# First block: the depthwise convolution wholly on TensorE in two halves, softmax in place in four buffers, layer norm sums inside the last two pairs of heads

## What is computed

```python
h = rms_norm(x, norm1_g);  a, gate, q, k, v = split(h @ w_in)
u = a * sigmoid(gate)                                # (256, 512)
y = depthwise_conv(u, dw_kernel, width=31) + dw_bias # centred, over tokens
y = silu(layer_norm(y, conv_ln_g, conv_ln_b))        # over the 512 channels
q, k = rms_norm per head;  8 heads of 64
p = softmax(q k^T / 8 + learned bias inside a 16-column window)
x = x + concat([y, p v]) @ w_out
x = x + (silu(h2 @ w_gate) * (h2 @ w_up)) @ w_down   # h2 = rms_norm(x, norm2_g)
```

## Time and profile before

| What | Value |
|---|---|
| Median of 3 runs | 1096.16 us (1095.68 to 1097.02) |
| Profiled execution | 1097.69 us, its span 1095.9 us |
| PE busy in the span | 1056.6 us (96%) |
| DVE, ACT, POOL busy | 680.8, 526.3, 69.6 us |
| Mean granted TensorE clock | 0.983 of full |
| DMA | 183.94 MB, mean 168 GB/s |
| Chain that ended last | PE 90%, DVE 4%, ACT 3%, DMA 1%, issue 1% |

### The profile page before, as it was taken

How to read it: one execution, slowest core, us unless ns; L and a number is a source line. 1 busy time by engine, 2 the same in 40 slices (tenths; PEclk the granted TensorE clock), 3 DMA queues, 4 the chain that set the end, 5 groups by cost and what they waited for, 6 DMA issues and landing times.

```text
span 1095.9 us, 19080 instructions
## 1 busy us (share of the span) xinstructions
PE 1056.6 (96%) x7498; PEld 972.8 (89%) x7501; DVE 680.8 (62%) x1035; ACT 526.3 (48%) x681; POOL 69.6 (6%) x80
## 2 busy tenths in 40 slices
PE   6997799999999999999999999989999999999997
PEld 5984589999998999999899899889999989999996
DVE  5995556555555677758655554565767676555554
ACT  6464554434445643546544444365344556444433
POOL 0000000000000115300000000003080000000000
PEclk7999899999999999999999999999999999999999
DMA  9971145455554655238465554645542584656520
GB/s 294 275 223 40 38 146 200 157 190 193 189 164 135 204 162 155 78 115 300 128 226 194 189 185 132 204 150 185 168 141 67 176 296 137 210 170 202 166 93 39
DMA packets 140146, 183.94 MB, mean 168 GB/s; under 512 B 5861, under 2 KB 125367, under 8 KB 140087
## 3 DMA queue, kind: packets, MB, share of 16 engines
q1 hardware_dynamic: 139576, 182.99, 52.8%
q10 hardware_dynamic: 511, 0.14, 0.1%
HBM read 180.90 MB, written 1.56 MB: 167 GB/s over the span
## 4 chain that ended last, share of the span: by engine, by line
PE 90%; DVE 4%; ACT 3%; DMA 1%; issue 1%; SPq 0%; ACTq 0%; DVEq 0%
PE col L490 19%; PE col L491 19%; PE col L492 19%; PE acc L490 9%; PE acc L491 9%; PE acc L492 9%; DVE wlo L1204 2%; ACT whi L900 1%; PE acc L661 1%; DVE y L1310 1%; DMA raw<-in_w_in 1%; PE acc L648 1%; PE acc L627 1%; PE col L679 1%; PE acc L557 1%
## 5 line engine op out<-in xcount | busy, mean ns | idle before, releaser
L1204 DVE TENSOR_TENSOR wlo<-raw,whi 128x2048 fp32r<-128x2048 f32 (+1 forms) x179 | 390.0, 2181 | 198.0 <-ACT whi L900 196.9
L490 PE MATMUL col<-uhi,whi 128*128 128x256 f32 (+1 forms) x1392 | 398.6, 286 | 4.7 <-DVE ulo L1231 3.9
L492 PE MATMUL col<-uhi,wlo 128*128 128x256 f32 (+1 forms) x1392 | 395.7, 284 | 0.0
L491 PE MATMUL col<-ulo,whi 128*128 128x256 f32 (+1 forms) x1392 | 395.7, 284 | 0.0
L900 ACT ACTIVATE whi<-raw 128x2048 fp32r<-128x2048 f32 (+1 forms) x179 | 325.0, 1820 | 121.6 <-PE acc L492 71.9
L490 PEld LDWEIGHTS col<-uhi,whi 128*128 128x128 f32 (+1 forms) x1392 | 267.6, 192 | 9.5 <-issue 6.0
L491 PEld LDWEIGHTS col<-ulo,whi 128*128 128x128 f32 (+1 forms) x1392 | 267.8, 192 | 1.5
L492 PEld LDWEIGHTS col<-uhi,wlo 128*128 128x128 f32 (+1 forms) x1392 | 267.8, 192 | 0.0
L490 PE MATMUL acc<-whi,mhi 128*128 128x512 f32 x376 | 148.5, 395 | 6.4 <-DVE wlo L1204 6.3
L491 PE MATMUL acc<-wlo,mhi 128*128 128x512 f32 x376 | 147.2, 392 | 0.0
L492 PE MATMUL acc<-whi,mlo 128*128 128x512 f32 x376 | 146.9, 391 | 0.0
(11 more groups left out here) (246 smaller groups left out, 1033.0 us busy)
## 6 DMA issues: line engine op xcount, KB each, us to landing
raw<-in_w_in SPq DMA_DIRECT2D x52, 1024.0 KB, 5.4
raw<-in_w_mlp_up SPq DMA_DIRECT2D x32, 1024.0 KB, 5.7
raw<-in_w_mlp_down SPq DMA_DIRECT2D x32, 1024.0 KB, 4.9
raw<-in_w_gate SPq DMA_DIRECT2D x11, 1024.0 KB, 5.4
raw<-in_w_up SPq DMA_DIRECT2D x11, 1024.0 KB, 5.4
raw<-in_w_down SPq DMA_DIRECT2D x11, 1024.0 KB, 4.8
raw<-in_w_mix_out SPq DMA_DIRECT2D x8, 1024.0 KB, 5.7
raw<-in_w_out SPq DMA_DIRECT2D x4, 1024.0 KB, 9.6
```

The lines of the kernel that those rows point to most:

```text
L490: pe.matmul(out, l_hi, r_hi, start=start, stop=False)
L491: pe.matmul(out, l_hi, r_lo, start=False, stop=False)
L492: return pe.matmul(out, l_lo, r_hi, start=False, stop=stop)
L1204: dve.tensor_tensor(wlo[:, u.buf, 0:size], raw[:, u.slot, 0:size], whi[:, u.buf, 0:size].bitcast(F32), ALU.subtract).then_inc(w_lo, 1)
```

## The change

All four chunks of the convolution go to PE, in two halves of two chunks with the same `shifted` and `kst` buffers. The first half's shift copies are issued by SP between the loads of units 8 and 9, and its 64 matmuls follow unit 6 on PE. The second half's copies wait for the first half's matmuls and follow the load of unit 11; its stationaries are built by DVE after unit 8's turn in its list; its matmuls lie in pairs 0 and 1. The taps of DVE are gone. The tap gathers move from ACT's queue to SP's, behind unit 1, and carry twice the rows; their transpose stands after unit 0. Softmax runs in place: maximum, exponential and scaling use the same one of four buffers, and ACT no longer waits for a turn before an exponential. The mean's matmuls move into pair 2, the variance's into pair 3, the subtraction and the squares beside them. ACT splits unit 12 before the pairs and unit 13 right after the sigmoids; DVE's low halves stay after the pairs and after the convolution's low halves. ACT's own load of the square root's table before the wait for the variance is dropped. `last_rows` asks for units 12 and 13 and their inputs one after the other.

The core of the diff:

```diff
             load(a_unit(0), w_in[:, :, A_COLS[0]:A_COLS[0] + COLS])
             for j in range(1, A_OUT):
                 load(a_unit(j), w_in[:, :, A_COLS[j]:A_COLS[j] + COLS])
+                if j == 1:
+                    for s in range(SHIFTS):
+                        n = (TAPS - s + SHIFTS - 1) // SHIFTS
+                        sp.dma_start(krow[0:GROUPS * n, SHIFT_CH * s:SHIFT_CH * s + SHIFT_CH], taps_of(s, n)).then_inc(taps_in, 16)
+                    sp.dma_start(krow[GROUPS * (TAP_SETS - 1):GROUPS * TAP_SETS, SHIFT_CH * (SHIFTS - 1):P], taps_of(TAPS - 1, 1))\
+                        .then_inc(taps_in, 16)
+                if j == 8:
+                    shift(0)
...
+            def shift(half):
+                sp.wait_ge(glu, half + 1)
+                if half:
+                    sp.wait_ge(conv_ps, 2)
+                for s in range(SHIFTS):
+                    for q in range(SHIFTS):
...
                 load(a_unit(A_OUT + i), w_out[:, 2 * r:2 * r + 2, :])
                 if i == 1:
...
+                    shift(1)
...
+            def convolve(c):
+                for g in range(TAP_SETS):
                     for q in range(SHIFTS):
+                        mm = pe.matmul(CONV_BANK[c][SHIFT_CH * q:SHIFT_CH * q + SHIFT_CH, 0:T], kst[2 * (c % 2) + q // 2][:, g, q % 2, :],
+                                       shifted[:, SHIFTS * (c % 2) + q, SHIFTS * g:SHIFTS * g + T], start=g == 0, stop=g == TAP_SETS - 1)
+                mm.then_inc(conv_ps, 1)
...
+                if j == 0:
+                    tap_transposes()
+                if j == 6:
+                    pe.wait_ge(kst_ok, 1)
+                    pe.wait_ge(shift_in, 16 * SHIFTS * SHIFTS)
+                    convolve(0)
+                    convolve(1)
                 if j == 7 or j == 8:
                     n = j - 7
                     pe.wait_ge(qk_tok, n + 1)
+                    if n:
+                        pe.wait_ge(conv_sb, 2)
                     turn((qtok, ktok)[n], n)
             for p in range(HEADS // 2):
                 if p + 1 < HEADS // 2:
                     score_pair(0, p + 1)
                 if p == 0:
                     pe.wait_ge(evac, A_OUT)
-                    pe.wait_ge(kst_ok, 1)
-                    pe.wait_ge(shift_in, 16 * SHIFTS * SHIFTS)
+                    pe.wait_ge(kst_ok, 2)
+                    pe.wait_ge(shift_in, 2 * 16 * SHIFTS * SHIFTS)
                 else:
                     value_pair(0, p - 1)
-                if p < len(CONV_AT):
-                    convolve(CONV_AT[p - 1] if p else 0, CONV_AT[p])
+                if p < 2:
+                    convolve(2 + p)
+                elif p == 2:
+                    pe.wait_ge(conv_sb, KA)
+                    for c in range(KA):
+                        mm = pe.matmul(MU[:, 0:T], ones[:], y[:, c, :], start=c == 0, stop=c == KA - 1)
+                    mm.then_inc(ln_mu, 1)
+                else:
+                    pe.wait_ge(ln_sq, 2)
+                    for c in range(KA):
+                        mm = pe.matmul(VAR[:, 0:T], ones[:], lnsq[:, c, :], start=c == 0, stop=c == KA - 1)
+                    mm.then_inc(ln_var, 1)
                 turn_probs(0, 2 * p)
                 turn_probs(0, 2 * p + 1)
...
             def exps(a, h):
                 act.wait_ge(s_max, HEADS * a + h + 1)
-                if h >= 2:
-                    act.wait_ge(p_ps, HEADS * a + h - 1)
                 for t in range(NT):
+                    p = expo[h % 4][:, t, 0:keys(a, t)]
+                    act.activation(p, p, ACT.Exp, bias=nmx[:, h % 4, t:t + 1], accum_out=den[:, h % 4, t:t + 1]).then_inc(s_exp, 1)
...
+                    if j == 0:
+                        act.wait_ge(kx_ps, 1)
+                        act.activation(kx[:], col[2][:, 0:TAP_SETS * GROUPS], ACT.Copy).then_inc(kx_sb, 1)
...
             exps(0, 1)
+            split(a_unit(A_OUT + 2))
             for p in range(HEADS // 2):
...
                     if e == 0 and p >= 1:
                         o_split(0, p - 1)
-            o_split(0, 3)
-            for p in range(2):
-                f = slice(2 * p, 2 * p + 2)
-                act.wait_ge(ln_xc, p + 1)
-                act.activation(lnsq[:, f, :], y[:, f, :], ACT.Square).then_inc(ln_sq, 1)
-            split(a_unit(A_OUT + 2))
-            act.activation(sd[:, 2:3], eps[:, 0:1], ACT.Sqrt)
+                for c in range(2 if p == 2 else 0):
+                    f = slice(2 * c, 2 * c + 2)
+                    act.wait_ge(ln_xc, c + 1)
+                    act.activation(lnsq[:, f, :], y[:, f, :], ACT.Square).then_inc(ln_sq, 1)
             act.wait_ge(ln_var, 1)
             act.activation(lnsd, VAR[:, 0:T], ACT.Sqrt, bias=eps[:, 0:1]).then_inc(ln_sd, 1)
+            o_split(0, 3)
             act.activation(sd[:, 3:4], eps[:, 0:1], ACT.Sigmoid)
...
+            split(a_unit(A_OUT + 3))
             for p in range(2):
                 act.wait_ge(c_ok, p + 1)
...
             def softmax_max(a, h):
                 dve.wait_ge(s_ps, HEADS * a + h + 1)
-                if h >= 2:
-                    dve.wait_ge(s_exp, NT * (HEADS * a + h - 1))
+                if h >= 4:
+                    dve.wait_ge(p_ps, HEADS * a + h - 3)
...
                 if j == 1:
-                    tap_stationaries()
-                convolve(TAPS_AT[j])
+                    tap_stationaries(0)
+                if j == 7:
+                    conv_evac(0)
+                    conv_evac(1)
+                if j == 8:
+                    tap_stationaries(1)
...
                 if p >= 1:
                     o_split(0, p - 1)
+                if p < 2:
+                    conv_evac(2 + p)
+                for c in range(2 if p == 2 else 0):
+                    f = slice(2 * c, 2 * c + 2)
+                    if c == 0:
+                        dve.wait_ge(ln_mu, 1)
+                    dve.tensor_tensor(y[:, f, :], y[:, f, :], MU[:, 0:T].unsqueeze(1).broadcast_to([P, 2, T]), ALU.subtract)\
+                        .then_inc(ln_xc, 1)
             split(a_unit(A_OUT + 2))
             dve.wait_ge(ln_sd, 1)
             link(dve.reciprocal(lnr, lnsd))
             for c in range(KA):
                 dve.tensor_tensor(y[:, c, :], y[:, c, :], lnr, ALU.mult).then_inc(ln_y, 1)
+                if c == 0:
+                    o_split(0, 3)
```

More of the change, by code:

```diff
@@ L191, in build @@
         rn = sb("rn", [P, 16])
[L192 to L195, removed]
+        mx = sb("mx", [P, 4, NT])
+        nmx = sb("nmx", [P, 4, NT])
+        den = sb("den", [P, 4, NT])
+        rden = sb("rden", [P, 4, NT])
         rni = sb("rni", [P, NT])
@@ L208, in build @@
         xnt = xn[:].rearrange("p (t a) b -> p t (a b)", t=NT)
-        score = [xn[:, 0, :].rearrange("p (t k) -> p t k", t=NT), xn[:, 1, :].rearrange("p (t k) -> p t k", t=NT)]
-        expo = [xn[:, 2, :].rearrange("p (t k) -> p t k", t=NT), xn[:, 3, :].rearrange("p (t k) -> p t k", t=NT)]
+        expo = [xn[:, b, :].rearrange("p (t k) -> p t k", t=NT) for b in range(4)]
         iqtok = y[:, 0:2, :]
@@ L223, in build @@
         diag = rtmp[:, 0:2, :]
[L224 to L228, removed]
+        spread = big[:].rearrange("p a b -> p (a b)")[:, HEADS * BIAS_ROW:HEADS * BIAS_ROW + HALF_GROUPS * SHIFTED]
+        shifted = spread.rearrange("p (r x) -> p r x", r=HALF_GROUPS)
+        mask32 = itmp[:, 0, 0:SHIFT_CH]
         kst = [v.rearrange("p a b -> p (a b)").rearrange("p (g r m) -> p g r m", g=TAP_SETS, r=2)
@@ L284, in build @@
         o_lo = sem("o_lo")
-        conv_dve = sem("conv_dve")
+        taps_in = sem("taps_in")
+        kx_ps = sem("kx_ps")
+        kx_sb = sem("kx_sb")
         kst_ok = sem("kst_ok")
@@ L420, in _, with taps_of @@
                 sp.dma_start(x[:, t, :], d["x"][0, t * P:(t + 1) * P, :]).then_inc(x_in[t], 16)
+            def shift(half):
[4 more added lines that the diff above has]
+                    for q in range(SHIFTS):
+                        into = shifted[SHIFT_CH * s:SHIFT_CH * s + SHIFT_CH, :, :].rearrange("p (c q) x -> p c q x", q=SHIFTS)
+                        sp.dma_start(into[:, :, q, :], cu[SHIFT_CH * q:SHIFT_CH * q + SHIFT_CH, 2 * half:2 * half + 2, s:s + SHIFTED])\
+                            .then_inc(shift_in, 16)
+            def taps_of(w, n):
+                return bass.AP(tensor=d["params"].tensor, offset=(G_N + w * KA) * P,
+                               ap=[[SHIFTS * KA * P, n], [SHIFT_CH, GROUPS], [1, SHIFT_CH]])
             load(a_unit(0), w_in[:, :, A_COLS[0]:A_COLS[0] + COLS])
@@ L559, in turn_quarter, with last_rows @@
                         tr.then_inc(u_ps, 1)
-            def last_rows(parts, k=None):
+            def last_rows(parts, k=None, ready=None):
                 for i, (t, h) in enumerate(QUARTERS):
@@ L565, in last_rows @@
                     for n, (u, hi_in, lo_in) in enumerate(parts):
+                        if i == 0 and ready:
+                            ready(n)
```

(32 more changed lines are left out.)

100 lines of the change are left out of this document (18 added, 82 removed).

## The result

The changed kernel takes 1086.64 us (median of 4, 1084.12 to 1087.15) beside 1095.92 for before: ratio 0.9912 [0.9892, 0.9932]. It is 9.3 us faster, where 17.9 were forecast, and lies above the range's upper end of 1086.0. Once more, on another chip: 1084.89 beside 1097.12, ratio 0.9893 [0.9878, 0.9908]. That second time would lie inside the range, but the forecast's ratio, 1078.3 / 1096.16 = 0.984, lies outside both intervals. The profiled execution took 1086.87 us.

A forecast was written before the change was run, and what follows sets the result against it. PE was taken as the bound, with waits and a low clock before 160 us; 0.4 before the pairs, 7.6 in them, 1.7 in units 10 and 11, 6.5 wait, 1.7 clock: 17.9 saved, 1078.3 us, range 1075.5 to 1086.

The forecast's parts named there:

- the last rows: On PE after units 10 and 11: 48 x 0.2275 plus two quarter turns, 11.8 us, ending at 132.3 against 150.2.
- The step that failed: Convolution on PE, before and in the pairs: a chunk of 32 matmuls costs 1.82 us, two chunks 3.64.
- Mean and variance: In the pairs on PE: 8 matmuls each at 1.53 us, 3.06 together.
- Rival B: The clock falls again, in pair 3's gap of 1.9 us, costing up to 3.4 us: 1081.7; chance 0.15.
- Shift copies: On SP: 16 issued in 11.46 us per half, 3 us to landing, all hidden; unit 12 behind them +3.1 at worst.
- Rival C: SP's shift copies take longer each and delay PE; at 2 us each, 26.9 us later, 1105.2; chance 0.03.
- The gathers: Five tap gathers moved to SP's queue: 3.0 to 8.9 us of SP, effect between -0.4 and +2, taken as 0.
- the pairs' gaps: PE's waits inside the pairs: 2.5 us with the handoffs, of which 1.9 in pair 3.
- the helpers' chain: ACT and DVE after the pairs: PE waits 0.5 us in unit 10 for O_BANK; later splits level or early.
- rival A: After the pairs, the helper chain on ACT and DVE ends last: +3 us, 1081.3; chance 0.17.
- units 10 and 11: On PE after the pairs: 5.46 us each, plus value pair 1.01 and a wait of 0.5, 12.4 together.
- The table load: On ACT behind the last copy: 1.28 us without a drain; the skill's 2.7 would add 1.1 at the end, 1079.4.

The follow-up runs named there:

- e13: The changed kernel with the convolution's chunk 0 computed four times in all behind unit 6: 1095.94 us, ratio 0.9985 to before.
- e7: The changed kernel with eight matmuls of zeros on PE ahead of pair 3's value pair, filling PE's wait: 1084.58 us, ratio 0.9888 to before.
- e9: The changed kernel with head 5's probabilities copied on ACT ahead of head 7's exp, cutting pair 3's wait in two: 1086.6 us, ratio 0.9909 to before.
- e2: Before with the four in-place softmax buffers and the layer norm's sums in the pairs, the convolution as before: 1084.79 us, ratio 0.9893.
- e11: The changed kernel with chunk 0's taps on DVE and eight matmuls of zeros in pair 3's gap: 1081.58 us, ratio 0.9866 to before.
- e12: As e11, but ACT copies head 5 and does the squares before head 7's exp; four and two zero matmuls in two gaps: 1081.22 us, ratio 0.9859.
- e14: As e2, plus eleven matmuls of zeros on PE during its wait for the first row maximum: 1082.31 us, ratio 0.9873 to before.

## Why the prediction was wrong

The direction and the waits were right, the size was not. The profiled time was forecast at 1079.8 and came at 1086.87; at the end of the last rows the trace is 7.7 us behind the forecast, and 0.6 came back after it.

- **The step that failed** is "48 take 2.73 us, so a chunk of 32 is 1.82 and two chunks 3.64". The 48 are records, 24 matmuls. A chunk costs 3.6 (e13). This term stands twice in the sum, ahead of the pairs (3.64 for 7.05) and in them (3.64 for 7.19): 7.0 us. A check was at hand: before's own three pieces, from 88.30, 95.88 and 103.74, last 2.73, 2.73 and 1.86, together 7.3 for the two chunks it has there. With the price right the same sum gives 139.3 for the end. A second check: laid over before's own pairs (86.38 to 116.11, 29.7), the sum's terms for scores, chunks, value pairs and turns give 16.5. Its mean adds 1.5, its waits 5.0, and its low clock 2.8 (value pair, turns and mean, from 109.71 to 116.11, took 6.4 where the terms have 3.6): 25.8. The 3.9 that lack are about the 3.7 by which two chunks were priced too low.
- **Mean and variance** went in at 1.53 each, the one row that I took; at full clock they take 1.83 here. That is 0.6. (Their "8 matmuls" are 8 records of 4 matmuls too; no harm came of it, since the duration was taken whole.)
- **Rival B came**: the clock fell in pair 3 behind a wait of 1.98 us. Price 1.6 (value pair 0.7, variance 0.9), within the 3.4 given as its most; in the traces of e7 and e9, with the wait filled or cut in two, it is gone. I gave it 0.15.
- **Not foreseen, the other way**: unit 0 began 1.9 us sooner than in before's trace, 1.2 in the mean over traces. I had bounded this edit at -0.4.
- **Shift copies**: 12.3 and 10.3 us of SP for 11.46 each; the first half landed 0.6 us too late in this trace and in time in the repeat's, where it took SP 13.2. Rival C did not decide.
- **The gathers** took SP 6.8 us for five and delayed nothing that PE wanted. Here the estimate stood.
- **The rest**: of the pairs' gaps 2.0 came for 2.5; the helpers' chain was 0.3 late once for 0.5 forecast, so rival A did not come; units 10 and 11 and the last rows are within 0.6 of the forecast together.
- **The table load** now stands behind the last copy, as forecast, and again has its ACTIVATE at once behind it (ACT's timeline, changed kernel):

```profile
116.38 1.28 ACT L1077 ACT_TABLE_LOAD   x1
117.67 0.48 ACT L1077 ACTIVATE xn<-col,eps 128x256 f32<-128x256 f32 x1
```

The Trainium skill (ScalarE: Activation LUTs, What ACT_TABLE_LOAD costs) adds a drain to it; no row here shows one.

The sum of the steps: +7.0 for the chunks, +0.6 for mean and variance, +1.6 for the clock and +0.6 for the late copies, less 1.9 for unit 0, comes to 7.9 us beside the 7.7 measured, so the account is nearly closed.

Which part earned the time: sums in the pairs 9.5 us alone, buffers 4.5 alone, both 12.7 in e2 (medians), and all the convolution's rework nothing that can be measured.

## What to carry to other kernels

Before a duration is divided by a count, check the count against the code: the profile may give one matmul of the source several records, and then the duration of a whole chunk is safe and its division is not. Lay a sum of terms over the kernel before, where the answer is known, before it is used for the changed one. Moving work from an engine with idle time to the one that bounds pays only for the waits that it removes; price both, and try moving the half that the idle engine can carry. And where PE waits for about 2 us or more, price the low clock behind the wait as a term with a chance, not as a rival.

## What was not expected of the hardware

- The clock's fall behind a gap is not the same every time: behind 1.98 us in pair 3 it fell in 8 of 10 profiles, behind 2.7 us ahead of pair 0 in 2 of 4 that left that gap open. Two gaps of 1.07 and 0.86 with PE at work between them left it at 1.00 (e9).
- A bf16 matmul of 128x512 with zeros took 0.24 us (1.89 for eight) and such matmuls in a gap went with a clock of 1.00 behind it in all four profiles that had them (e7, e11, e12, e14).
- Five gathers of short runs moved from ACT's to SP's queue let the first unit of weights be in use 1.2 us sooner in the mean (0.7 and 0.9 in the kernel that differs in nothing else), though nothing waited for the issuing engine.
